# Who multiplies the modulation blocks by silu(c): VectorE before, GpSimd between its splits of the weights after

## The chip, the cores and the metric

One core of one Trainium2 chip runs the whole program in one launch. The metric is the device time of that core in microseconds (us), given as the median of the runs made. TensorE (PE) multiplies matrices into eight PSUM banks, VectorE (DVE), ScalarE (ACT) and GpSimd (POOL) work elementwise, and SyncE (SP) issues nearly all loads from HBM to SBUF. Each engine runs its own program in order, and they meet only through counting semaphores.

## The reference, cut to what matters

Four transformer-like layers follow each other over 512 tokens of width 1024. The first two are modulated by a conditioning vector `c` of 1024 numbers:

```python
def adaln(c, w_mod, b_mod):
    mod = jax.nn.silu(c) @ w_mod + b_mod      # (1, 1024) @ (1024, 6144)
    return jnp.split(mod, 6, axis=-1)

def layer_ab(x, c, ...):
    sh_m, sc_m, g_m, sh_f, sc_f, g_f = adaln(c, mod_w, mod_b)
    h = modulate(x, norm_mix, sh_m, sc_m)
    ...
    x = x + g_m[:, None, :] * (jnp.concatenate([y_a, y_b], axis=-1) @ w_out)
    h = modulate(x, norm_ffn, sh_f, sc_f)
    return x + g_f[:, None, :] * swiglu(h, wg, wu, wd)
```

So there are two products of a vector by a 1024x6144 matrix, one for each of the first two layers. All other matrix products are of 512 tokens by a weight matrix. Everything is float32.

## The kernel before, in words

**Panels.** All weights are cut into 378 panels of 128 output columns: a panel is 128 partitions by 8 blocks of 128 (512 KB). A matrix product in float32 is made of three products of rounded parts (`three`, L567 to L569): high by high, low by high, high by low. A panel is 8 x 3 = 24 matmuls of 128x512. For each panel p, SP loads `raw` (L475), ACT rounds it into `w_hi` (`split_hi`, L902), POOL subtracts to get `w_lo` (`split_lo`, L518), and PE multiplies (`panel`). `raw`, `w_hi` and `w_lo` have RING = 4 slots each. SP loads panel p + 4 once `lo_ready` says that panel p is split; ACT rounds panel p once PE has done panel p - 4.

**Modulation blocks.** The two modulation matrices are 96 blocks q of the same shape as a panel. The first 16 are loaded at the start into `first_mods` and are finished before the first panel: 10 of them go through VectorE, 6 through PE alone (`ALONE`). The other 80 are loaded into `modraw`, which has MRING = 2 slots, and are taken along beside the panels: `mods_beside(p)` gives two of them to each of the panels 0 to 5, and one to each of the panels 6 to 73. Block q is multiplied by silu(c) (`csil`, one number for each row of the matrix), in place, then summed over its 8 blocks k into `modsum` (4 slots), and one matmul with a column of ones (`mod_panel`, L582) sums over the partitions into column q of PSUM bank 7. Before the change, VectorE does both steps in `sum_mod`: the multiply is L1382, the sum L1387.

**Order on VectorE.** It works AHEAD = 2 panels in front: beside panel p it runs `sum_mods(p + 2)` and only then takes panel p out of its bank, by `copy_out` (L1175) in the input panels or `add_x` (L1230) in the projections. In the gate and up panels of the feed-forward part, both blocks of a pair come behind the pair's `prod` (L1271) and `g_lo` (L1286).

**Order on SP**, which the change does not touch, is written out:

```python
                    p = MOD_TWICE + j
                    load_raw(it * 4 + (p + RING), (p + RING) % RING, it * 4 + (p + 1))
                    load_mod(it * 4 + (q_first + j), (q_first + j) % MRING, it * 4 + summed(q_first + j - MRING))
```

The last argument of `load_raw` is what `lo_ready` must have reached, that of `load_mod` what `mod_summed` must have reached; `q_first` is the block beside panel 6. The loop for the panels 0 to 5 has the same order: first `load_raw(p + RING, after=p + 1)`, then the blocks of `mods_beside(p)`, each once block q - 2 is summed. Blocks 16 and 17 are loaded ahead of both.

**Stages.** Panels 0 to 17 are the input projection of layer 0 (16 and 17 together in `token_panels`), beside the causal convolution and the scan of the recurrent branch on VectorE (`lru_conv`, `lru_scan`); behind panel 15, VectorE lays out the blocks of the compression (`lay_blocks`) and PE multiplies them (`hidden`, L748). Attention follows, with no panel in it. Then come panels 18 to 25 (out projection, `project`), the norm (`rstd`, `norm_h`), and the feed-forward part: gate and up panels 26 to 41, down panels 42 to 49, gate and up 50 to 65, down 66 to 73, and the rest, 74 to 93, with no modulation block.

Of the kernel before, what the change touches and what calls it, by code (L numbers as in the profile page):

```python
# [15 lines left out]
ALU = mybir.AluOpType  # L16
# [3 lines left out]
P = 128  # L20
D = 1024
T = 512
KB = D // P
# [15 lines left out]
RING = 4  # L39
# [3 lines left out]
MRING = 2  # L43
# [9 lines left out]
P_OUT0 = P_VW + 1  # L53
# [8 lines left out]
P_AG = P_FFN1 + FFN_PANELS  # L62
# [50 lines left out]
def build(nc, A):  # L113
    with ExitStack() as ctx:
# [11 lines left out]
        def sem(name):  # L126
            return ctx.enter_context(nc.semaphore(name))
# [142 lines left out]
        panel_done = sem("panel_done")  # L270
        bank_free = sem("bank_free")
        mod_summed = sem("mod_summed")
        mod_used = sem("mod_used")
        csil_ready = sem("csil_ready")
        squares_ready = sem("squares_ready")
# [237 lines left out]
        @block.gpsimd  # L513
        def _(pool):
            def split_lo(p, slot):

                pool.wait_ge(hi_ready, p + 1)
                pool.tensor_tensor(w_lo[:, slot, :], raw[:, slot, :], w_hi[:, slot, :].bitcast(F32), ALU.subtract)\  # L518
                    .then_inc(lo_ready, 1)

            def split_from(p0, n):
                with pool.Fori(0, n // RING) as it:
                    for j in range(RING):
                        split_lo(it * RING + (p0 + j), (p0 + j) % RING)
                for p in range(p0 + n // RING * RING, p0 + n):
                    split_lo(p, p % RING)

            split_from(0, P_OUT0 + RING)

            pool.wait_ge(cmp_done, 2)  # L530
            pool.wait_ge(bank_free, P_OUT0)
            for br, src in enumerate((ksT, kwT)):
                for b in range(2):
                    pool.tensor_scalar(k0pad[:, br, b, :], src[:, :], own_half[:, b:b + 1], None, ALU.mult)
            pool.drain()
            pool.sem_inc(keys_padded, 1)
            split_from(P_OUT0 + RING, P_AG - P_OUT0 - RING)

            pool.wait_ge(layer2_landed, 48)
            pool.affine_select(out=wsT[:, :, :], in_=wsT[:, :, :], compare_op=ALU.is_ge, fill=0.0, base=0,  # L540
                               pattern=[[0, 8], [1, P]], channel_multiplier=-1).then_inc(ws_masked, 1)
            split_from(P_AG, P_U + RING - P_AG)

            for p in range(P_U + RING, P_OUT2 + RING):
                split_lo(p, p % RING)
                for k in taps_beside(p - RING):
                    pool.wait_ge(tap_made, k)
                    pool.tensor_tensor(cout[:, 3, :], cout[:, 3, :], tapped[:, k % 2, :], ALU.add).then_inc(tap_added, 1)
                    pool.drain()
            split_from(P_OUT2 + RING, P_OUT3 - P_OUT2)  # L550

            pool.wait_ge(bank_free, P_OUT3)
            for g_ in range(2 * KB):
                if g_ >= 2:

                    pool.wait_ge(score_ready, U_AT[2] + 4 * (g_ - 1))
                for b in range(2):
                    pool.tensor_scalar(k3pad[:, g_ % 2, b, :], k3[:, g_ % KB, :], own_half[:, b:b + 1], None, ALU.mult)
                pool.drain()
                pool.sem_inc(keys_padded, 1)  # L560
            split_from(P_OUT3 + RING, N_PANELS - P_OUT3 - RING)
# [605 lines left out]
        def _(dve):  # L1167
# [207 lines left out]
                                         in1=cols[:, own:own + KB], op0=ADD, op1=MUL)  # L1375
                dve.drain()

            def sum_mod(panel_, landed, landed_value, used, sum_slot):

                dve.wait_ge(landed, landed_value)  # L1380
                w = panel_.rearrange("p (k n) -> p k n", n=P)
                dve.tensor_tensor(w, w, csil[:, :].rearrange("p (k o) -> p k o", o=1).broadcast_to((P, KB, P)), MUL)  # L1382
                dve.drain()

                if used is not None:
                    dve.wait_ge(mod_used, used)
                dve.tensor_reduce(modsum[:, sum_slot, :], panel_.rearrange("p (k n) -> p n k", n=P), AX_X, ADD)\  # L1387
                    .then_inc(mod_summed, 1)

            def first_sums():  # L1390
                dve.wait_ge(csil_ready, 1)
                by_dve = [q for q in range(MOD_FIRST) if q not in ALONE]
                for n, q in enumerate(by_dve):
                    sum_mod(first_mods[q // 4][:, q % 4, :], first_landed[q // 4], 16,
                            by_dve[n - SUMS] + 1 if n >= SUMS else None, summed(q) % SUMS)

            def sum_mods(p):

                for q in mods_beside(p):
                    sum_mod(modraw[:, q % MRING, :], mod_landed[q % MRING], 16 * ((q - MOD_FIRST) // MRING + 1),  # L1400
                            q - SUMS + 1, summed(q) % SUMS)

            def sum_mod_loop(it, p):

                q = mods_beside(p)[0]
                sum_mod(modraw[:, q % MRING, :], mod_landed[q % MRING], it * 32 + 16 * ((q - MOD_FIRST) // MRING + 1),
                        it * 4 + (q - SUMS + 1), summed(q) % SUMS)


# [546 lines left out]
```

## Time and profile before

| | |
|---|---|
| median of 3 runs | 2950.18 us (2949.32 to 2954.04) |
| profiled execution | span of 2948.6 us from the first to the last instruction; no time of its own is listed beside the three runs |
| PE busy | 2599.6 us, 88% of the span |
| DVE busy | 1508.2 us, 51% |
| POOL busy | 1012.6 us, 34% |
| ACT busy | 920.0 us, 31% |
| POOL, the 378 splits (L518) | 929.5 us, 2465 ns each |
| DVE, 80 multiplies by silu(c) (L1382) | 132.7 us, 1658 ns each |
| DVE, 80 sums over k (L1387) | 159.1 us, 1989 ns each |
| modulation blocks end at | 772 us of the span |

Busy shares are means over the whole span; a stage is read from the windows and the timeline. Matmuls overlap, so the pace of a panel is the distance between the same row of two panels and not the sum of its matmuls. In a timeline a row ends with the idle time in front of it and what ended that, in brackets.

### The profile page before, as it was taken

What the parts mean: (1) busy time and instruction counts of PE and PEld (TensorE: products, weight loads), DVE (VectorE), ACT (ScalarE), POOL (GpSimd) and SP (SyncE); (2) the same over time, 40 slices, a digit from 0 to 9 for tenths busy, and PEclk for the clock granted to TensorE, in tenths of its full rate; (3) what the DMA queues carried; (4) which work ended last, traced back from release to release, by engine and by line L of the source; (5) the groups of instructions that cost most, each with busy time, mean ns of one, the idle gap of its engine ahead of it and who ended that gap; (6) DMA issues with size and microseconds to landing.
All of it is one profiled execution on the core that took longest, in us unless ns stands there. A gap on an engine that the chain in (4) does not pass through costs nothing.

```text
span 2948.6 us, 36164 instructions
## 1 busy us (share of the span) xinstructions
PE 2599.6 (88%) x12106; PEld 2114.6 (72%) x12106; DVE 1508.2 (51%) x2628; ACT 920.0 (31%) x1481; POOL 1012.6 (34%) x435
## 2 busy tenths in 40 slices
PE   4678898999989888999996817999998988899998
PEld 4568676787876776788885706788876867688886
DVE  6993567686423873211116983525245435452534
ACT  2140453322233263322233223423232245342222
POOL 1130003444442202344452612344443353343443
PEclk9895899999998999999997958999999999999999
DMA  6431003455331102232231202232332210122322
GB/s 252 164 135 65 1 16 133 173 178 184 123 107 50 65 1 86 72 99 94 93 107 57 72 14 64 79 95 90 100 101 71 79 44 1 64 91 95 100 88 76
DMA packets 71769, 263.76 MB, mean 89 GB/s; under 512 B 7920, under 2 KB 8560, under 8 KB 71024
## 3 DMA queue, kind: packets, MB, share of 16 engines
q1 hardware_dynamic: 68352, 251.01, 25.9%
q10 hardware_dynamic: 3312, 11.40, 1.1%
q8 instruction: 60, 0.98, 0.1%
q14 instruction: 45, 0.37, 0.0%
HBM read 260.28 MB, written 2.10 MB: 89 GB/s over the span
## 4 chain that ended last, share of the span: by engine, by line
PE 50%; issue 30%; DVE 8%; POOL 7%; DVEq 2%; ACT 2%; POOLq 1%; DMA 0%; SPq 0%; ACTq 0%
PE bank L567 15%; PE bank L568 14%; PE bank L569 14%; POOL w_lo L518 7%; DVE cout L1693 2%; PE bank L680 2%; PE bank L670 1%; PE bank L661 1%; DVE tn L1219 1%; DVE acc L1192 1%; ACT prob L983 1%; DVE h_lo L1214 1%; PE bank L824 1%; DVE modsum L1387 1%; DVEq L1686 1%
## 5 line engine op out<-in xcount | busy, mean ns | idle before, releaser
L518 POOL TENSOR_TENSOR w_lo<-raw,w_hi 128x1024 fp32r<-128x1024 f32 x378 | 929.5, 2465 | 1821.4 <-ACT w_hi L902 1820.6
L567 PE MATMUL bank<-h_hi,w_hi 128*128 128x512 f32 x2128 | 862.2, 405 | 53.2 <-DVE h_lo L1214 40.4
L568 PE MATMUL bank<-h_lo,w_hi 128*128 128x512 f32 x2128 | 840.5, 395 | 0.0
L569 PE MATMUL bank<-h_hi,w_lo 128*128 128x512 f32 x2128 | 839.3, 394 | 0.0
L902 ACT ACTIVATE w_hi<-raw 128x1024 fp32r<-128x1024 f32 x378 | 397.4, 1055 | 759.7 <-PE bank L569 719.5
L567 PEld LDWEIGHTS bank<-h_hi,w_hi 128*128 128x128 f32 x2128 | 406.1, 191 | 172.1 <-DVE h_lo L1214 48.1
L569 PEld LDWEIGHTS bank<-h_hi,w_lo 128*128 128x128 f32 x2128 | 406.5, 191 | 87.3
L568 PEld LDWEIGHTS bank<-h_lo,w_hi 128*128 128x128 f32 x2128 | 407.3, 191 | 84.3 <-issue 4.6
L567 PE MATMUL bank<-g_hi,w_hi 128*128 128x512 f32 x704 | 280.6, 399 | 5.8 <-DVE g_lo L1286 5.8
L568 PE MATMUL bank<-g_lo,w_hi 128*128 128x512 f32 x704 | 278.6, 396 | 0.0
L569 PE MATMUL bank<-g_hi,w_lo 128*128 128x512 f32 x704 | 278.5, 396 | 0.0
L947 ACT ACTIVATE g_hi<-prod 128x512 f32 x88 | 55.6, 632 | 460.3 <-DVE prod L1283 242.9
L1271 DVE TENSOR_TENSOR prod<-silu,bank 128x512 f32<-128x512 f32 x44 | 30.3, 688 | 292.4 <-PE bank L569 292.4
L1230 DVE SCALAR_TENSOR_TENSOR x<-bank,plain,x 128x512 f32<-128x512 f32 x64 | 48.0, 751 | 257.6 <-PE bank L569 257.6
L1387 DVE TENSOR_REDUCE modsum<-modraw 128x128 f32<-128x1024 f32 x80 | 159.1, 1989 | 8.6 <-issue 0.6
L567 PEld LDWEIGHTS bank<-g_hi,w_hi 128*128 128x128 f32 x704 | 132.4, 188 | 39.7 <-DVE g_lo L1286 8.4
L569 PEld LDWEIGHTS bank<-g_hi,w_lo 128*128 128x128 f32 x704 | 132.5, 188 | 32.3
L568 PEld LDWEIGHTS bank<-g_lo,w_hi 128*128 128x128 f32 x704 | 132.5, 188 | 31.3
L1382 DVE TENSOR_TENSOR modraw<-modraw,csil 128x1024 f32<-128x1024 f32 x80 | 132.7, 1658 | 6.6 <-DMA modraw<-in_mods 6.3
L1230 DVE SCALAR_TENSOR_TENSOR x<-bank,modv,x 128x512 f32<-128x512 f32 x64 | 47.7, 746 | 165.5 <-PE bank L569 165.5
L1693 DVE SCALAR_TENSOR_TENSOR cout<-pad,cols,cout 128x512 f32<-128x512 f32 x104 | 116.1, 1144 | 4.7 <-issue 0.4
L983 ACT ACTIVATE prob<-srow,stat 128x512 f32<-128x512 f32 (+1 forms) x192 | 106.5, 555 | 31.9 <-DVE stat L1348 31.7
(236 smaller groups left out, 2985.8 us busy)
## 6 DMA issues: line engine op xcount, KB each, us to landing
raw<-in_panels SPq DMA_DIRECT2D x378, 512.0 KB, 3.5
modraw<-in_mods SPq DMA_DIRECT2D x80, 512.0 KB, 3.5
first_mods<-in_mods SPq DMA_DIRECT2D x4, 2048.0 KB, 20.4
w<-in_w ACTq DMA_DIRECT2D x2, 2048.0 KB, 9.2
x<-in_x SPq DMA_DIRECT2D x1, 2048.0 KB, 8.5
out<-yout ACTq DMA_DIRECT2D x8, 256.0 KB, 2.2
mask<-in_causal ACTq DMA_DIRECT2D x1, 1024.0 KB, 4.8
mask<-in_dilated ACTq DMA_DIRECT2D x1, 1024.0 KB, 4.9
```

Source lines behind the costliest of these rows:

```text
L518: pool.tensor_tensor(w_lo[:, slot, :], raw[:, slot, :], w_hi[:, slot, :].bitcast(F32), ALU.subtract)\
L567: pe.matmul(out, w_h, m_h, start=start, stop=False)
L568: pe.matmul(out, w_h, m_l, start=False, stop=False)
L569: return pe.matmul(out, w_l, m_h, start=False, stop=stop)
L680: m = pe.matmul(bank[4 + n % 2][:, 0:HD], probT[:, n % 2, P * j:P * j + P], v_of(run, units[n], j), start=(j == 0), stop=(j == last))
L902: act.activation(w_hi[:, slot, :], raw[:, slot, :], ACT.Copy).then_inc(hi_ready, 1)
L947: act.activation(g_hi[:, it * 2 + a, :], prod[:, a, :], ACT.Copy).then_inc(f_hi_ready, 1)
L983: act.activation(prob[:, n % 3, 0:w], srow[:, n % 2, 0:w], ACT.Exp, bias=stat[:, 0, u % 64:u % 64 + 1], scale=SCALE, accum_out=stat[:, 1, ...
L1230: dve.scalar_tensor_tensor(out=x[:, n, :], in0=bank[p % RING][:, :], scalar=scale_by, in1=x[:, n, :], op0=MUL, op1=ADD).then_inc(bank_free, 1)
L1382: dve.tensor_tensor(w, w, csil[:, :].rearrange("p (k o) -> p k o", o=1).broadcast_to((P, KB, P)), MUL)
L1387: dve.tensor_reduce(modsum[:, sum_slot, :], panel_.rearrange("p (k n) -> p n k", n=P), AX_X, ADD)\
L1693: dve.scalar_tensor_tensor(out=cout[:, c, :], in0=pad[:, c, k:k + T], scalar=col("cconv", 4 * k + c), in1=cout[:, c, :], op0=MUL, op1=ADD)
```

## The change: GpSimd multiplies, VectorE sums

GpSimd's program gets a multiply of block q by `csil` behind the split of the panel that the block stands beside (`split_and_scale`, and `split_and_scale_from` as a loop of 4), with a wait on the block's load. A new semaphore `mod_scaled` counts these multiplies, and VectorE's sum waits for it in place of the load. The first 16 blocks stay as they were (`scale_first`). GpSimd also waits once, at the start, for `csil`.

```diff
--- before.py
+++ after.py
@@ -270,6 +270,7 @@
         panel_done = sem("panel_done")
         bank_free = sem("bank_free")
         mod_summed = sem("mod_summed")
+        mod_scaled = sem("mod_scaled")
         mod_used = sem("mod_used")
         csil_ready = sem("csil_ready")
         squares_ready = sem("squares_ready")
@@ -525,7 +526,34 @@
                 for p in range(p0 + n // RING * RING, p0 + n):
                     split_lo(p, p % RING)
 
-            split_from(0, P_OUT0 + RING)
+            def scale_mod(q, slot, landed):
+
+                pool.wait_ge(mod_landed[slot], landed)
+                w = modraw[:, slot, :].rearrange("p (k n) -> p k n", n=P)
+                pool.tensor_tensor(w, w, csil[:, :].rearrange("p (k o) -> p k o", o=1).broadcast_to((P, KB, P)), ALU.mult)\
+                    .then_inc(mod_scaled, 1)
+
+            def split_and_scale(p):
+
+                split_lo(p, p % RING)
+                for q in mods_beside(p):
+                    scale_mod(q, q % MRING, 16 * ((q - MOD_FIRST) // MRING + 1))
+
+            def split_and_scale_from(p0, n):
+
+                q0_ = mods_beside(p0)[0]
+                with pool.Fori(0, n // RING) as it:
+                    for j in range(RING):
+                        split_lo(it * RING + (p0 + j), (p0 + j) % RING)
+                        q = q0_ + j
+                        scale_mod(q, q % MRING, it * 32 + 16 * ((q - MOD_FIRST) // MRING + 1))
+                for p in range(p0 + n // RING * RING, p0 + n):
+                    split_and_scale(p)
+
+            pool.wait_ge(csil_ready, 1)
+            for p in range(MOD_TWICE):
+                split_and_scale(p)
+            split_and_scale_from(MOD_TWICE, P_OUT0 + RING - MOD_TWICE)
 
             pool.wait_ge(cmp_done, 2)
             pool.wait_ge(bank_free, P_OUT0)
@@ -534,7 +562,8 @@
                     pool.tensor_scalar(k0pad[:, br, b, :], src[:, :], own_half[:, b:b + 1], None, ALU.mult)
             pool.drain()
             pool.sem_inc(keys_padded, 1)
-            split_from(P_OUT0 + RING, P_AG - P_OUT0 - RING)
+            split_and_scale_from(P_OUT0 + RING, MOD_UNTIL - P_OUT0 - RING)
+            split_from(MOD_UNTIL, P_AG - MOD_UNTIL)
 
             pool.wait_ge(layer2_landed, 48)
             pool.affine_select(out=wsT[:, :, :], in_=wsT[:, :, :], compare_op=ALU.is_ge, fill=0.0, base=0,
@@ -1375,13 +1404,17 @@
                                          in1=cols[:, own:own + KB], op0=ADD, op1=MUL)
                 dve.drain()
 
-            def sum_mod(panel_, landed, landed_value, used, sum_slot):
-
-                dve.wait_ge(landed, landed_value)
+            def scale_first(panel_, landed):
+
+                dve.wait_ge(landed, 16)
                 w = panel_.rearrange("p (k n) -> p k n", n=P)
                 dve.tensor_tensor(w, w, csil[:, :].rearrange("p (k o) -> p k o", o=1).broadcast_to((P, KB, P)), MUL)
                 dve.drain()
 
+            def sum_mod(panel_, scaled, used, sum_slot):
+
+                if scaled is not None:
+                    dve.wait_ge(mod_scaled, scaled)
                 if used is not None:
                     dve.wait_ge(mod_used, used)
                 dve.tensor_reduce(modsum[:, sum_slot, :], panel_.rearrange("p (k n) -> p n k", n=P), AX_X, ADD)\
@@ -1391,19 +1424,20 @@
                 dve.wait_ge(csil_ready, 1)
                 by_dve = [q for q in range(MOD_FIRST) if q not in ALONE]
                 for n, q in enumerate(by_dve):
-                    sum_mod(first_mods[q // 4][:, q % 4, :], first_landed[q // 4], 16,
+                    scale_first(first_mods[q // 4][:, q % 4, :], first_landed[q // 4])
+                    sum_mod(first_mods[q // 4][:, q % 4, :], None,
                             by_dve[n - SUMS] + 1 if n >= SUMS else None, summed(q) % SUMS)
 
             def sum_mods(p):
 
                 for q in mods_beside(p):
-                    sum_mod(modraw[:, q % MRING, :], mod_landed[q % MRING], 16 * ((q - MOD_FIRST) // MRING + 1),
+                    sum_mod(modraw[:, q % MRING, :], q - MOD_FIRST + 1,
                             q - SUMS + 1, summed(q) % SUMS)
 
             def sum_mod_loop(it, p):
 
                 q = mods_beside(p)[0]
-                sum_mod(modraw[:, q % MRING, :], mod_landed[q % MRING], it * 32 + 16 * ((q - MOD_FIRST) // MRING + 1),
+                sum_mod(modraw[:, q % MRING, :], it * 4 + (q - MOD_FIRST + 1),
                         it * 4 + (q - SUMS + 1), summed(q) % SUMS)
```

GpSimd's program, in its loop of four splits for the panels 0 to 19, before:

```order
L518 TENSOR_TENSOR w_lo<-raw,w_hi 128x1024 [waits hi_ready]
L517 REGISTER_ALU
L518 TENSOR_TENSOR w_lo<-raw,w_hi 128x1024 [waits hi_ready]
L517 REGISTER_ALU
L518 TENSOR_TENSOR w_lo<-raw,w_hi 128x1024 [waits hi_ready]
L517 REGISTER_ALU
L518 TENSOR_TENSOR w_lo<-raw,w_hi 128x1024 [waits hi_ready]
```

and after, panels 0 and 1, which carry two modulation blocks each:

```order
L519 TENSOR_TENSOR w_lo<-raw,w_hi 128x1024 [waits hi_ready,csil_ready]
L533 TENSOR_TENSOR modraw<-modraw,csil 128x1024 [waits mod_landed0]
L533 TENSOR_TENSOR modraw<-modraw,csil 128x1024 [waits mod_landed1]
L519 TENSOR_TENSOR w_lo<-raw,w_hi 128x1024 [waits hi_ready]
L533 TENSOR_TENSOR modraw<-modraw,csil 128x1024 [waits mod_landed0]
L533 TENSOR_TENSOR modraw<-modraw,csil 128x1024 [waits mod_landed1]
```

In its loop for the panels from 6 on, with one block each, after:

```order
L519 TENSOR_TENSOR w_lo<-raw,w_hi 128x1024 [waits hi_ready]
L531 ISA
L533 TENSOR_TENSOR modraw<-modraw,csil 128x1024 [waits mod_landed0]
L518 REGISTER_ALU
L519 TENSOR_TENSOR w_lo<-raw,w_hi 128x1024 [waits hi_ready]
L533 TENSOR_TENSOR modraw<-modraw,csil 128x1024 [waits mod_landed1]
L518 REGISTER_ALU
L519 TENSOR_TENSOR w_lo<-raw,w_hi 128x1024 [waits hi_ready]
```

Between any two splits there is now one multiply, or two, each with a wait for a load into its slot of `modraw`.

VectorE's program, from the last `h_lo` of the first norm to the first panel taken out, before:

```order
L1214 SCALAR_TENSOR_TENSOR h_lo<-tn,modv,h_hi 128x512 [waits h_hi_ready] x2
L1382 TENSOR_TENSOR modraw<-modraw,csil 128x1024 [waits mod_landed0]
L1387 TENSOR_REDUCE modsum<-modraw 128x128 [waits mod_used]
L1382 TENSOR_TENSOR modraw<-modraw,csil 128x1024 [waits mod_landed1]
L1387 TENSOR_REDUCE modsum<-modraw 128x128 [waits mod_used]
L1382 TENSOR_TENSOR modraw<-modraw,csil 128x1024 [waits mod_landed0]
L1387 TENSOR_REDUCE modsum<-modraw 128x128 [waits mod_used]
L1382 TENSOR_TENSOR modraw<-modraw,csil 128x1024 [waits mod_landed1]
L1387 TENSOR_REDUCE modsum<-modraw 128x128 [waits mod_used]
L1382 TENSOR_TENSOR modraw<-modraw,csil 128x1024 [waits mod_landed0]
```

and after:

```order
L1243 SCALAR_TENSOR_TENSOR h_lo<-tn,modv,h_hi 128x512 [waits h_hi_ready] x2
L1420 TENSOR_REDUCE modsum<-modraw 128x128 [waits mod_used,mod_scaled] x6
L1204 COPY axp<-bank 128x512 [waits panel_done]
L1420 TENSOR_REDUCE modsum<-modraw 128x128 [waits mod_used,mod_scaled] x2
L1204 COPY axp<-bank 128x512 [waits panel_done]
L1420 TENSOR_REDUCE modsum<-modraw 128x128 [waits mod_used,mod_scaled] x2
L1204 COPY axp<-bank 128x512 [waits panel_done]
```

The multiplies are gone from between the sums, and each sum waits for `mod_scaled`, GpSimd's count. SP's program has the same rows before and after.

## Rows read from the trace of the kernel before

**Rows 1.** Five stretches: length, busy PE PEld DVE ACT POOL (instructions), PEclk, DMA share, GB/s.

```profile
core 0 of [0], span 2948.6 us
...
80.00:245.00 165.00, 118.04 (x493) 95.30 (x494) 152.78 (x121) 45.07 (x52) 39.32 (x16) 0.82 0.41 137
...
425.00:473.00 48.00, 46.49 (x206) 38.37 (x204) 38.01 (x29) 12.69 (x15) 17.47 (x8) 0.96 0.43 149
473.00:498.00 25.00, 14.55 (x47) 9.70 (x48) 16.38 (x26) 10.14 (x14) 1.95 (x1) 0.73 0.15 52
498.00:772.00 274.00, 272.64 (x1217) 220.20 (x1216) 201.54 (x139) 68.84 (x81) 126.03 (x47) 1.00 0.51 173
772.00:870.00 98.00, 98.00 (x431) 80.29 (x430) 18.09 (x26) 30.89 (x39) 47.81 (x20) 1.00 0.34 105
```

**Rows 2.** Windows of L1382 alone: length, DVE busy (instructions), PEclk, DMA share, GB/s.

```profile
...
80.00:245.00 165.00, 42.37 (x26) 0.82 0.41 137
...
```

**Rows 3.** Timeline, second down projection: start us, us, engine, line.

```profile
603.78 2.40 POOL L518 TENSOR_TENSOR w_lo<-raw,w_hi 128x1024 fp32r<-128x1024 f32 x1 [3.42 <-ACT w_hi L902]
604.08 3.18 DVE L1382 TENSOR_TENSOR modraw<-modraw,csil 128x1024 f32<-128x1024 f32 x1
607.33 2.00 DVE L1387 TENSOR_REDUCE modsum<-modraw 128x128 f32<-128x1024 f32 x1
608.26 0.28 PE L582 MATMUL bank<-ones,modsum 128*128 128x1 f32 x2
609.25 0.73 DVE L1230 SCALAR_TENSOR_TENSOR x<-bank,modv,x 128x512 f32<-128x512 f32 x1
614.08 0.28 PE L582 MATMUL bank<-ones,modsum 128*128 128x1 f32 x2
```

**Rows 4.** Timeline, out projection: the split of panel 22 and what it releases.

```profile
433.09 2.66 POOL L518 TENSOR_TENSOR w_lo<-raw,w_hi 128x1024 fp32r<-128x1024 f32 x1 [121.27 <-ACT w_hi L902]
435.92 0.33 SPq L475 DMA_DIRECT2D raw<-in_panels  x1
436.51 0.33 SPq L482 DMA_DIRECT2D modraw<-in_mods  x1
440.90 1.23 DVE L1382 TENSOR_TENSOR modraw<-modraw,csil 128x1024 f32<-128x1024 f32 x1 [2.53 <-DMA modraw<-in_mods]
```

**Rows 5.** Loads of modraw, 425 to 500 us.

```profile
...
DMA to landing us min/median/max: 4.1/4.3/4.8
```

**Rows 6.** Loads of modraw, 590 to 640 us.

```profile
...
DMA to landing us min/median/max: 3.4/3.4/3.9
```

**Rows 7.** Timeline of VectorE, start and end of the input panels.

```profile
81.13 1.22 DVE L1382 TENSOR_TENSOR modraw<-modraw,csil 128x1024 f32<-128x1024 f32 x1
221.84 1.87 DVE L1387 TENSOR_REDUCE modsum<-modraw 128x128 f32<-128x1024 f32 x1
223.62 0.68 DVE L1175 COPY kwT<-bank 128x512 f32<-128x512 f32 x1
```

**Rows 8.** Timeline of TensorE, the first products of the compression.

```profile
230.58 13.89 PE L748 MATMUL bank<-blocks,w 128*128 128x64 f32 x64 [26.47 <-issue]
```

**Rows 9.** Timeline of VectorE: last row of the out projection; g_lo of panels 26, 27.

```profile
472.90 0.74 DVE L1230 SCALAR_TENSOR_TENSOR x<-bank,modv,x 128x512 f32<-128x512 f32 x1
504.31 0.69 DVE L1286 TENSOR_TENSOR g_lo<-prod,g_hi 128x512 f32 x1 [0.93 <-ACT g_hi L947]
```

**Rows 10.** Timeline of GpSimd, the split of panel 30.

```profile
498.62 2.38 POOL L518 TENSOR_TENSOR w_lo<-raw,w_hi 128x1024 fp32r<-128x1024 f32 x1 [23.68 <-ACT w_hi L902]
```

**Rows 11.** Timeline of TensorE, the last modulation matmul, then panel 74.

```profile
772.10 0.28 PE L582 MATMUL bank<-ones,modsum 128*128 128x1 f32 x2
```

**Rows 12.** Timeline of TensorE, two matmuls in a row behind an idle stretch.

```profile
115.35 0.63 PE L568 MATMUL bank<-h_lo,w_hi 128*128 128x512 f32 x1
115.78 0.63 PE L569 MATMUL bank<-h_hi,w_lo 128*128 128x512 f32 x1
```

**Rows 13.** Instructions of L548: ns min/median/max.

```profile
L548 POOL TENSOR_TENSOR cout<-cout,tapped x16: 1507/1710/1841, 1650.6 to 1706.5; 128x512 f32<-128x512 f32 x16
```

## The prediction

> **What bounds the kernel now.** I first took the windows by stage. In the input panels (80 to 245 us) VectorE is busy for 152.8 of 165 us and TensorE for 118.0: VectorE sets the pace there [rows 1]. From 498 to 772 us TensorE is busy for 272.6 of 274 us at full clock, with VectorE at 201.5 and GpSimd at 126.0 [rows 1]: a wait of VectorE costs nothing there. The reader should see that the multiplies leave a tight VectorE in the first stretch only: 42.4 us in 26 instructions [rows 2].
>
> Then the pace of a panel. The modulation matmul that ends a panel stands at 608.26 and the next at 614.08 us: 5.82 us a panel [rows 3]. Within them GpSimd splits once, 2.40 us. Its period therefore has 3.4 us free, and a multiply as long as a split would fit by busy time: 4.8 us in 5.82. What decides is not the busy time but what each instruction waits for, so I followed one modulation block from the split to its first use.
>
> The split of panel 22 runs from 433.09 for 2.66 us, to 435.75. SyncE then issues the load of `raw` at 435.92 and that of `modraw` at 436.51, and VectorE's multiply, which waits for it, begins at 440.90 [rows 4]. So from the end of a split to the arrival of the block that stands beside the same panel there are **5.15 us**: 0.76 to issue, 4.4 to land. The loads of this stretch, issued in such pairs, landed in 4.1 to 4.8 us [rows 5]; loads issued apart from a `raw` load took 3.4 us [rows 6]. In the kernel before nobody feels this, since VectorE uses block q(p) two panels behind the split of p, and GpSimd does not wait for it.
>
> **What the change makes of it.** GpSimd now runs split(p), multiply q(p), split(p + 1), in this order. Multiply q(p) waits for a load that SyncE issues only once `lo_ready` has counted split(p). GpSimd therefore waits out each load, with the next split queued behind the wait. Its period is 2.40 (split) + 5.2 (issue and landing) + 2.4 (multiply) = **10.0 us a panel**, against 5.7 to 5.8 for TensorE. TensorE cannot begin panel p before split(p). The two slots of `modraw` don't help, as the order of SyncE's program and not a lack of slots holds the load back.
>
> The multiply on GpSimd is not in the trace. It has the size and the number of inputs of a split, so I take the split's 2.40 us [rows 3]. Its lower bound is the same 2.40, since no row shows GpSimd faster on that size. Its upper bound is 3.0 to 3.7: twice the 1.51 to 1.84 us of GpSimd's in-place 128x512 addition [rows 13], of which part is waiting for VectorE. The Trainium skill (GPSIMD Engine Reference, Performance versus the Vector engine) gives about 2.6 cycles an element for two inputs at 1.2 GHz, an estimate of 2.2 us for 1024; with it the sum would be 14 us lower over 72 multiplies. The split's own 2.40 us, above it, decides.
>
> For the wait I take 5.2 us. The bounds are 4.2 (0.76 + 3.4, if it lands like a load issued apart) and 5.6 (0.76 + 4.8).
>
> *Input panels.* GpSimd gets through split 0, both blocks, split 1, and then waits for block 18, whose load needs block 16 summed; that is behind the norm, as before. VectorE is free at 81.1 [rows 7]. It sums block 16 (2.0), the load lands 3.5 later at 86.6, two multiplies end at 91.4 (the second load lands meanwhile), and split(2) begins there. Panels 2 to 5 with two blocks take 2.4 + 5.2 + 4.8 = 12.4 each, 49.6 together, to 141.0; panels 6 to 17 take 10.0 each, 120, to 261.0; with the sum, 263.0. Before, the same sum ended at 223.7 (221.84 + 1.87), followed by the copy and the layout that let `hidden` begin at 230.58 [rows 7, 8]. That is **+39.3 us**. The multiplies taken off VectorE give nothing back, since it now waits for GpSimd: per panel its sum, copy and scan, some 7 us, lie inside the 10. The blocks of panels 18 to 21 are multiplied under `hidden`, the token panels and the attention, where GpSimd was idle; nothing is late there.
>
> *Out projection* (times as before, without the 39.3). Split(22) ends at 435.75 as before, as its `w_hi` waits for panel 18. Multiply 22 ends at 443.35 and each further one 10.0 later: that of panel 27 at 493.35, its sum at 495.35. `sum_mods(27)` stands ahead of `add_x(25)`, the last row of the projection, which began at 472.90 [rows 9]. Nothing of the norm can begin without it: **+22.4 us**. The splits themselves stay ahead of TensorE up to panel 25, so the projection loses nothing else. During the norm GpSimd catches up with panels 28 and 29; its rows may hold up an `h_lo` of the norm once, some 2 us, which I leave out of the sum.
>
> *Feed-forward.* Split(30) waits for panel 26: 498.62 before [rows 10], 521.0 now, to 523.4. Its block needs the sum of block q(28), which stands behind `g_lo` of panel 27 (504.31 + 0.69 before [rows 9], 527.4 now): sum to 529.4, load to about 533.0, multiply to 535.4, split(31) to 537.8. From there 10.0 each: split(74) ends at 537.8 + 430 = 967.8. TensorE's three panels of lead are used up at about panel 34. Panel 74, the first without a block, began behind the modulation matmul of 772.10 [rows 11], so 195.7 of which 22.4 is counted: **+173.3 us**. From 74 on split follows split in 2.4 us and TensorE is at its old pace. `prod`, `g_lo` and `add_x` run later behind their sums, by under 10 us, while a bank is needed again only four panels later; they hide there. Nothing after 93 touches the change.
>
> Sum: 39.3 + 22.4 + 173.3 = 235 us over the span of 2948.6. The median of the runs is 1.6 us above that span, so 2950.2 + 235 = **3185 us**, 8% slower.
>
> **The rivals.**
>
> *VectorE's relief shows (faster).* If a block were there when its split ends, GpSimd would need 4.8 us a panel and keep up, and the stretch from 80 to 245 us would lose up to the 42.4 us of multiplies [rows 2]: 2908 us. It turns at a wait of 0.9 us (5.7 less 4.8). Against it stand 5.15 us in [rows 4] and a SyncE program that has not moved. 2%; that the relief and the waits cancel within the measurement, 1%.
>
> *GpSimd's multiply is dearer*: in place and with a repeated operand it may go like the additions of [rows 13], at 3.1 us. With 22 multiplies in series in the input panels, 6 in the projection and 44 in the feed-forward, 72 x 0.7 = 50: 3235 us. 11%.
>
> *The block lands sooner*, at 4.2 us behind the split: 16 + 6 + 43 = 65 waits x 1.0: 3120 us. Fewer loads run at once than before, which speaks for it; the pair of loads issued together, as in [rows 5], against. 8%.
>
> *TensorE's clock becomes the limit.* It is starved for 4 us in each 10. Behind an idle stretch two matmuls start 0.43 us apart [rows 12], the level of 1.2 GHz, and the granted clock was 0.82 in the stretch where TensorE idled 28% of the time [rows 1]. If it stayed at the low level, a panel would take 24 x 0.43 + 0.3 = 10.6, over the 10.0, and the 40 panels from 34 on would add 0.6 each less the lead: 3205 us. The Trainium skill (TensorE: Matmul & The Clock Gate, The HAM clock gate) says that the throttled state is the default and activity releases it, which would allow this. 6%.
>
> The Trainium skill (GPSIMD Engine Reference, Key points) also says that GpSimd shares its SBUF interfaces with VectorE instructions that have two SBUF inputs. The multiply of VectorE that met a split took 3.18 us [rows 3] and the free one 1.22 [rows 7]. That speaks against the change, but with VectorE waiting anyway it moves no term.
>
> **How the numbers follow.** The forecast gets 72%: 3185 us. The range runs from 3125 to 3250: low end at the shorter wait, high end at the dearer multiply with a little of the longer wait (65 x 0.4 = 26). A measurement here can tell 0.2%, 6 us. Faster by more than that: 0.02; within: 0.01; slower: 0.97.
>
> **What would show it.** GpSimd's idle time ahead of its new multiply should be some 5 us, ended by the load of `modraw`, about 65 times; the gap between two splits 10.0 us from panel 34 to 73; VectorE idle ahead of its sums, ended by GpSimd; TensorE at about 55% from 560 to 1000 us, waiting for `w_lo`; `hidden` at about 270 us, panel 74 at about 1007. The forecast is wrong if the splits follow each other in under 6 us, or if SyncE's load of `modraw` is issued ahead of the split beside it.

## The result, and the profile after

| | before | after |
|---|---|---|
| median of the runs | 2951.86 us (4 runs, 2949.32 to 2954.04) | 3156.78 us (4 runs, 3147.57 to 3162.48) |
| profiled execution | span 2948.6 us | span 3145.8 us, time 3147.57 us |
| PE busy | 2599.6 us | 2662.9 us |
| DVE busy | 1508.2 us | 1364.0 us |
| POOL busy | 1012.6 us | 1144.6 us |
| mean granted clock | 0.930 | 0.912 |

The ratio is 1.0696, with an interval of 1.0676 to 1.0715: 7.0% slower. The forecast was 3185 us with a range of 3125 to 3250. The sign, the mechanism and the range held; the size is 28 us under the forecast.

The page of the kernel after, its groups of instructions (busy us and mean ns, then idle time ahead of them and what ended it):

```profile
L519 POOL TENSOR_TENSOR w_lo<-raw,w_hi 128x1024 fp32r<-128x1024 f32 x378 | 911.4, 2417 | 1499.6 <-ACT w_hi L931 1498.8
...
L1420 DVE TENSOR_REDUCE modsum<-modraw 128x128 f32<-128x1024 f32 x80 | 155.0, 1943 | 402.1 <-POOL modraw L533 401.6
L533 POOL TENSOR_TENSOR modraw<-modraw,csil 128x1024 f32<-128x1024 f32 x80 | 153.5, 1922 | 412.1 <-DMA modraw<-in_mods 412.1
```

VectorE lost its 132.7 us of multiplies and got 401.6 us of waiting for GpSimd. GpSimd got 153.5 us of multiplies and 412.1 us of waiting for the loads. The waits of the kernel after (total us, times, longest) show how regular that is, and how it goes on from engine to engine:

```profile
POOL modraw L533 <- DMA modraw<-in_mods: 412.1, 74, 23.1
DVE modsum L1420 <- POOL modraw L533: 401.6, 68, 8.1
...
PE bank L611 <- DVE modsum L1420: 134.6, 65, 4.1
```

One turn of the loop in GpSimd's timeline, second feed-forward part (start, length, and in brackets the idle time ahead):

```profile
598.90 2.36 POOL L519 TENSOR_TENSOR w_lo<-raw,w_hi 128x1024 fp32r<-128x1024 f32 x1
606.44 1.90 POOL L533 TENSOR_TENSOR modraw<-modraw,csil 128x1024 f32<-128x1024 f32 x1 [5.19 <-DMA modraw<-in_mods]
608.30 2.36 POOL L519 TENSOR_TENSOR w_lo<-raw,w_hi 128x1024 fp32r<-128x1024 f32 x1
615.72 1.90 POOL L533 TENSOR_TENSOR modraw<-modraw,csil 128x1024 f32<-128x1024 f32 x1 [5.06 <-DMA modraw<-in_mods]
```

And SyncE's queue between the first two of them:

```profile
601.43 0.33 SPq L476 DMA_DIRECT2D raw<-in_panels  x1
602.02 0.33 SPq L483 DMA_DIRECT2D modraw<-in_mods  x1
```

The split ends at 601.26, `raw` is issued 0.17 us later, `modraw` at 602.02, and the multiply begins at 606.44, 5.18 us behind the split. The next split stands behind it. This is the chain of [rows 4], now with GpSimd waiting inside it. From the split at 598.90 to that at 608.30 it takes 9.4 us. In the kernel before, a panel took 5.82 [rows 3].

The ends of the stages in the kernel after, from the timelines of TensorE, GpSimd, VectorE and TensorE again:

```profile
258.39 13.88 PE L777 MATMUL bank<-blocks,w 128*128 128x64 f32 x64 [24.75 <-issue]
```

```profile
452.17 2.40 POOL L519 TENSOR_TENSOR w_lo<-raw,w_hi 128x1024 fp32r<-128x1024 f32 x1 [122.02 <-ACT w_hi L931]
...
552.49 2.41 POOL L519 TENSOR_TENSOR w_lo<-raw,w_hi 128x1024 fp32r<-128x1024 f32 x1
...
953.52 2.35 POOL L519 TENSOR_TENSOR w_lo<-raw,w_hi 128x1024 fp32r<-128x1024 f32 x1
```

```profile
511.97 0.73 DVE L1259 SCALAR_TENSOR_TENSOR x<-bank,modv,x 128x512 f32<-128x512 f32 x1
```

```profile
965.41 0.49 PE L596 MATMUL bank<-h_hi,w_hi 128*128 128x512 f32 x1 [0.18 <-DVE x L1259]
```

- Input panels: `hidden` begins at 258.39 in place of 230.58 [rows 8], +27.8.
- From there to the split of panel 22: 452.17 in place of 433.09 [rows 4], so 8.7 us come back. The cause is below, in the section on what the runs showed.
- Out projection: its last row at 511.97 in place of 472.90 [rows 9], +39.1, of which 20.0 arose here.
- Feed-forward: panel 74 begins at 965.41. Before it began behind the modulation matmul of 772.10 [rows 11], at 772.24: +193.2, of which 154.1 arose here. The splits of panels 31 and 73 are 401.03 us apart, 42 periods of 9.55 us on average; single ones take 9.1 to 10.4.
- The rest: 197.2 - 193.2 = +4.0.

The windows of the kernel after, with the columns of [rows 1]:

```profile
80.00:245.00 165.00, 113.87 (x426) 86.55 (x426) 79.57 (x78) 45.06 (x51) 76.99 (x37) 0.84 0.35 119
560.00:960.00 400.00, 305.21 (x1096) 234.17 (x1095) 108.42 (x83) 60.59 (x71) 176.92 (x84) 0.86 0.32 110
```

No engine is full in either stretch. VectorE is busy for 79.6 us where it was busy for 152.8 [rows 1], the load share of 0.35 is lower too, and the time is longer. Between 560 and 960 us GpSimd has the highest share beside TensorE, and that is 44%. A loop of waits bounds the kernel, and only the timeline shows it.

### The profile page after: what moved, and what is told of

Its sections match the earlier page's. It is cut to its first block, busy times and chain, and to the rows that moved or that the text cites. A ratio compares the mean times of both kernels' runs of the same rounds, so it can differ in the third digit from the quotient of the medians.

```text
span 3145.8 us, 36170 instructions
## 1 busy us (share of the span) xinstructions
PE 2662.9 (85%) x12106; PEld 2149.4 (68%) x12106; DVE 1364.0 (43%) x2548; ACT 919.4 (29%) x1481; POOL 1144.6 (36%) x515
## 4 chain that ended last, share of the span: by engine, by line
PE 38%; issue 36%; POOL 14%; DVE 7%; DVEq 2%; ACT 2%; DMA 1%; POOLq 1%; ACTq 0%; SPq 0%
POOL w_lo L519 11%; PE bank L596 11%; PE bank L597 11%; PE bank L598 11%; POOL modraw L533 3%; DVE cout L1727 2%; PE bank L709 1%; PE bank L699 1%; PE bank L690 1%; DVE tn L1248 1%; DVE h_lo L1243 1%; ACT prob L1012 1%; PE bank L853 1%; DVE modsum L1420 1%; DMA modraw<-in_mods 1%
## 5 line engine op out<-in xcount | busy, mean ns | idle before, releaser
L519 POOL TENSOR_TENSOR w_lo<-raw,w_hi 128x1024 fp32r<-128x1024 f32 x378 | 911.4, 2417 | 1499.6 <-ACT w_hi L931 1498.8
L596 PE MATMUL bank<-h_hi,w_hi 128*128 128x512 f32 x2128 | 879.2, 413 | 54.7 <-DVE h_lo L1243 40.3
L597 PE MATMUL bank<-h_lo,w_hi 128*128 128x512 f32 x2128 | 855.5, 402 | 0.0
L598 PE MATMUL bank<-h_hi,w_lo 128*128 128x512 f32 x2128 | 853.1, 401 | 0.0
L596 PEld LDWEIGHTS bank<-h_hi,w_hi 128*128 128x128 f32 x2128 | 415.5, 195 | 177.8 <-DVE h_lo L1243 48.0
L598 PEld LDWEIGHTS bank<-h_hi,w_lo 128*128 128x128 f32 x2128 | 415.8, 195 | 91.2
L597 PEld LDWEIGHTS bank<-h_lo,w_hi 128*128 128x128 f32 x2128 | 416.7, 196 | 87.4 <-issue 4.7
L1420 DVE TENSOR_REDUCE modsum<-modraw 128x128 f32<-128x1024 f32 x80 | 155.0, 1943 | 402.1 <-POOL modraw L533 401.6
L533 POOL TENSOR_TENSOR modraw<-modraw,csil 128x1024 f32<-128x1024 f32 x80 | 153.5, 1922 | 412.1 <-DMA modraw<-in_mods 412.1
L611 PE MATMUL bank<-ones,modsum 128*128 128x1 f32 x180 | 35.5, 268 | 134.6 <-DVE modsum L1420 134.6
L611 PEld LDWEIGHTS bank<-ones,modsum 128*128 128x128 f32 x180 | 32.0, 214 | 159.7 <-issue 111.8
```

Of the source, the lines that this page charges most:

```text
L533: pool.tensor_tensor(w, w, csil[:, :].rearrange("p (k o) -> p k o", o=1).broadcast_to((P, KB, P)), ALU.mult)\
L596: pe.matmul(out, w_h, m_h, start=start, stop=False)
L597: pe.matmul(out, w_h, m_l, start=False, stop=False)
L598: return pe.matmul(out, w_l, m_h, start=False, stop=stop)
L611: pe.matmul(out, modsum[:, slot, :], ones[:, 0:1], start=True, stop=True).then_inc(mod_used, 1)
```

## The experiments

Each median below is set against runs of the kernel before that were made beside it on the same chip. The kernels of the first two experiments ran on one chip, those with the wait alone, the squared block and the two halves on a second, the rest on a third.

**The order of the two loads.** The first pair moves SyncE's load of the block ahead of that of `raw`, in both loops, in the kernel after and in the kernel before. A block's load then waits only for its slot, and no longer for the split beside it.

```diff
-                    load_raw(it * 4 + (p + RING), (p + RING) % RING, it * 4 + (p + 1))
                     load_mod(it * 4 + (q_first + j), ...
+                    load_raw(it * 4 + (p + RING), (p + RING) % RING, it * 4 + (p + 1))
```

In the kernel after:

> Only SyncE's order is changed against the kernel after: in each turn the load of the modulation block stands ahead of the load of raw, so it is no longer behind the wait for the split beside it. If the serial loop split, load, multiply is the cost, block q(p) is on its way while GpSimd multiplies the block before it and splits p: two panels take 2.4 + 5.2 + 1.9 = 9.5, 4.75 us a panel, under TensorE's 5.7, and all of the 205 us come back. The input panels may then show VectorE's relief, some 20 us: 2932 us, between 2915 and 2955. If the loss were GpSimd's own added work or the traffic on the SBUF ports, the time would stay over 3100 us.

In the kernel before:

> The same swap of the two loads in the kernel before, with VectorE still multiplying. VectorE uses a block two panels after its split, so an earlier load is worth little: 2952 us, within 6 of the kernel before. If the swap by itself were the gain of the run above, this one would be some 20 us faster too.

Measured: the changed kernel with the new order 2946.76 us (11 runs, 2937.03 to 2949.03), 0.9983 of before (0.9974 to 0.9992). The kernel before with the new order 2951.05 us (12 runs), 0.9998 (0.9989 to 1.0006). The order of two loads in SyncE's program takes back the whole 7%, and does nothing where GpSimd does not wait. The waits and a window of the changed kernel in the new order:

```profile
POOL modraw L533 <- DMA modraw<-in_mods: 120.7, 45, 23.2
```

```profile
80.00:245.00 165.00, 119.70 (x503) 97.81 (x504) 119.89 (x95) 46.74 (x53) 92.07 (x42) 0.82 0.44 146
520.00:780.00 260.00, 260.00 (x1174) 213.45 (x1173) 123.32 (x88) 64.95 (x76) 194.60 (x89) 1.00 0.53 178
```

In the feed-forward part TensorE is full at the full clock again, with GpSimd at 75%. This version beats both kernels, but the kernel before by only 0.17%. The relief of VectorE is in it (119.9 us busy for 152.8 of [rows 1]), but `hidden` begins at 228.60 for 230.58, where 33 us of VectorE's work are gone. Even these 2 us are no gain of the relief: in the kernel before with the new order, where VectorE still multiplies, `hidden` begins at 228.83. Where the relief went is the question of the last pair.

**One split between the load and its use.** GpSimd splits panel p + 1 before it multiplies the block beside p; SyncE stays as in the change.

```diff
+            split_lo(0, 0)
+            for p in range(P_OUT0 + RING):
+                if p + 1 < P_OUT0 + RING:
+                    split_lo(p + 1, (p + 1) % RING)
+                for q in mods_beside(p):
+                    scale_mod(q, q % MRING, 16 * ((q - MOD_FIRST) // MRING + 1))
```

(The same from panel 22 on.)

> SyncE's order as in the kernel after, but GpSimd multiplies the block beside panel p behind the split of panel p + 1, so that the load passes under a split. By the same sum two panels take 9.5 us: 4.75 a panel, TensorE sets the pace again, and the time is near that of the swap of the loads, 2920 to 2965 us. If not the wait but the multiply between two splits is what costs, it stays near 3157.

Measured: 2959.82 us (6 runs), 1.0031 of before (1.0019 to 1.0042). The loop is broken here too, at the other end, and 9.4 us remain. Where they come from, in the timelines of GpSimd, VectorE and TensorE:

```profile
258.70 2.34 POOL L519 TENSOR_TENSOR w_lo<-raw,w_hi 128x1024 fp32r<-128x1024 f32 x1 [38.53 <-ACT w_hi L938]
261.00 1.89 POOL L533 TENSOR_TENSOR modraw<-modraw,csil 128x1024 f32<-128x1024 f32 x1
```

```profile
262.93 1.91 DVE L1427 TENSOR_REDUCE modsum<-modraw 128x128 f32<-128x1024 f32 x1 [23.87 <-POOL modraw L533]
```

```profile
266.09 0.43 PE L801 MATMUL bank<-hid,w 128*64 128x32 f32 x4 [8.28 <-DVE vtok L1220]
```

The multiply of the block beside panel 19 now stands behind the split of panel 20, which waits until TensorE has done the token panels. VectorE holds its sum ahead of the copies that TensorE needs for the compression. That matmul ran at 258.81 in the trace of before: 7.3 us of the 9.4. The product behind it took 13.92 us for 12.01, most of the rest.

**The wait without the multiply.** GpSimd waits for the block and counts, and the product with silu(c) is left out.

```diff
-                pool.tensor_tensor(w, w, csil[:, :]..., ALU.mult)\
-                    .then_inc(mod_scaled, 1)
+                pool.sem_inc(mod_scaled, 1)
```

> The kernel after, where GpSimd waits for each of the 80 blocks and counts it, and multiplies none of them: the factor silu(c) is left out of these blocks. If the loop is serial, its period falls by the 1.90 us of the multiply, 72 times: 3157 - 137 = 3020 us, still 70 us slower than the kernel before, with nothing added but a wait. If the multiply's work were the whole cost, 2950 us.

Measured: 3040.95 us (4 runs) against 2949.88, 1.0300 (1.0283 to 1.0317). GpSimd's timeline:

```profile
603.67 2.36 POOL L519 TENSOR_TENSOR w_lo<-raw,w_hi 128x1024 fp32r<-128x1024 f32 x1 [5.70 <-DMA modraw<-in_mods]
611.44 2.41 POOL L519 TENSOR_TENSOR w_lo<-raw,w_hi 128x1024 fp32r<-128x1024 f32 x1 [5.42 <-DMA modraw<-in_mods]
```

The wait alone costs 91 us, with no new work on any engine. Its period is 7.8 us here, and 7.9 from panel 31 to 73, for 9.55 with the multiply: it falls by 1.6 to 1.7, where the multiply itself is 1.90, since the loads arrive a little later behind the split. Split 22 starts at 431.39 in this run, 1.7 us earlier than before [rows 4], and at 431.28 in a run below whose first 22 panels are as before: in the input panels, where VectorE was the bound, the wait by itself costs nothing, and all 91 us arise from panel 22 on. The other 116 us of the change (206.9, if its median is set against these runs of before) come with the multiplies that stand in the loop, on average 1.6 for each of the 72. The expected 3020 us, which gave each the full 1.90, was missed by 21 us.

**What a multiply costs there.** It took 1.90 us and the forecast had taken 2.40 from the split. Three kernels each changed one thing that differs between the two: the operand that is repeated (`csil`, replaced by `w`: the block is squared), the operation (subtract for multiply), and the type of the output.

```diff
-                pool.tensor_tensor(w, w, csil[:, :]..., ALU.mult)
+                pool.tensor_tensor(w, w, w, ALU.mult)
```

> The kernel after with the block multiplied by itself in place of the repeated csil, so silu(c) is left out and both operands are 1024 different elements. If the multiply took 1.90 and not 2.40 us because one operand stays the same for 128 elements, it now takes 2.40, and 72 of them in series add 36 us: 3193 us. If the type of the output or the operation made it cheaper, it stays at 1.90 and 3157 us.

```diff
-                pool.tensor_tensor(w, w, csil[:, :]..., ALU.mult)
+                pool.tensor_tensor(w, w, csil[:, :]..., ALU.subtract)
```

> The kernel after with subtract in place of multiply (the blocks become w - silu(c), so the factor is left out). The split is a subtraction and takes 2.36 to 2.40 us, the multiply 1.90. If the operation makes the difference, GpSimd's 80 instructions now take 2.4 us and the time rises by 72 x 0.5 to 3193. If the type of the split's output or its being out of place makes it, they stay at 1.90 us and the time at 3157.

```diff
-                pool.tensor_tensor(w, w, csil[:, :]..., ALU.mult)
+                pool.tensor_tensor(w.bitcast(F32R), w, csil[:, :]..., ALU.mult)
```

> The kernel after, with the multiply's output written as fp32r, the rounded type that the split writes, and nothing else changed. Two full operands and the subtraction both left the 1.90 us as they were; what is left of the difference to the split is its output: type, or written in another place. If the type makes it, the multiply takes 2.36 to 2.40 us, 72 of them in series add 35, and the time is 3190 us, nearer my forecast of 3185. If not, 1.90 us and 3155.

Measured: 3164.06, 3150.39 and 3155.36 us (4, 2 and 2 runs), 1.0714, 1.0676 and 1.0698 of before, with intervals of 0.2 to 0.3% to either side. The instruction itself (ns min/median/max), in the three kernels:

```profile
L533 POOL TENSOR_TENSOR modraw<-modraw x80: 1887/1893/2870, 56.4 to 979.5; 128x1024 f32<-128x1024 f32 x80
```

```profile
L533 POOL TENSOR_TENSOR modraw<-modraw,csil x80: 1889/1897/2877, 56.5 to 957.1; 128x1024 f32<-128x1024 f32 x80
```

```profile
L533 POOL TENSOR_TENSOR modraw<-modraw,csil x80: 1891/1899/2887, 56.3 to 972.1; 128x1024 fp32r<-128x1024 f32 x80
```

None of the three by itself is the reason: the median is 1.89 to 1.90 us each time. Two differences to the split (2417 ns mean in the kernel after) are left. The multiply writes over its own input, while the split reads two buffers and writes a third; and the code gives the multiply its block as 8 pieces of 128, the split its 1024 elements as one piece. Neither was tried by itself. That in place is quicker as such is doubtful: GpSimd's in-place addition takes 1.51 us at the least for half the elements [rows 13], though part of that may be waiting for VectorE. The reason stays open.

**Only half of the change.** In the first kernel GpSimd multiplies beside the panels 0 to 21 and VectorE from 22 on; in the second it is the other way round.

```diff
-            split_and_scale_from(P_OUT0 + RING, MOD_UNTIL - P_OUT0 - RING)
-            split_from(MOD_UNTIL, P_AG - MOD_UNTIL)
+            split_from(P_OUT0 + RING, P_AG - P_OUT0 - RING)
```

(VectorE's part, which in both kernels multiplies the blocks that GpSimd doesn't, is left out here.)

> GpSimd multiplies only the 28 blocks beside the panels 0 to 21; VectorE those beside 22 to 73, as in the kernel before. The loss of the input panels alone: the trace of the kernel after has hidden begin some 28 us later, so 2952 + 28 = 2980 us. If losses of the stages hid each other, it would differ from that.

```diff
-            for p in range(MOD_TWICE):
-                split_and_scale(p)
-            split_and_scale_from(MOD_TWICE, P_OUT0 + RING - MOD_TWICE)
+            split_from(0, P_OUT0 + RING)
```

> The converse: VectorE multiplies the 28 blocks beside the panels 0 to 21, GpSimd the 52 beside 22 to 73. 3157 - 28 = 3129 us, so that this loss and that of the run above add up to the whole 205.

Measured: 2982.6 us (4 runs), +32.7, 1.0114 (1.0097 to 1.0131); and 3130.55 us (4 runs), +180.7, 1.0615 (1.0598 to 1.0633). Together 213.4 us, for the 206.9 of the whole change. The two parts add, within the spread of some us between runs. `hidden` begins at 260.52 in the first and at 229.09 in the second, 31.4 us apart. In all, it begins at 258.4 to 261.0 in the five traces where GpSimd multiplies there with the old order of loads, and at 228.9 to 230.6 in the three where it doesn't. The +27.8 above, from two single traces, is thus the low end; the input panels lose 28 to 32 us.

**Where the relief of VectorE went.** The new order of loads comes again, once without the multiply (the product with silu(c) is left out, GpSimd waits and counts), and once whole, with GpSimd multiplying beside the panels 0 to 21 alone. Both edits are put together from those shown above: that of the loads, with that of the wait or that of the first half.

> The loads swapped as in e1_block_before_raw, and GpSimd only waits and counts, so the factor silu(c) is left out of the 80 blocks. It shows what VectorE's relief of 42 us is worth with nothing put on GpSimd. If GpSimd's multiplies give the relief back, because VectorE's instructions with two SBUF operands wait for them (the three taps of the first convolution took 7.37 us in e1 against 2.40), hidden begins at 215 to 220 us and the time is 2930 to 2937 us. If the relief is worth little because TensorE's pace and the chain of the scans set the end of the input panels, it stays at 2942 to 2947.

> The loads swapped, GpSimd multiplies beside the panels 0 to 21, VectorE from 22 on. From 22 on TensorE sets the pace whoever multiplies, so the gain of e1, if it is from the input panels, is kept: 2946 us, 2943 to 2950. If part of e1's gain were from the feed-forward stage, this is nearer 2950.

Measured: 2929.88 us (5 runs) against 2949.85, 0.9922 (0.9909 to 0.9936); and 2948.83 us (11 runs), 0.9986 (0.9976 to 0.9996). The first is 20.0 us under before, 19.0 under the second, which ran beside it, and 16.9 under the whole kernel in the new order, which ran on another chip. `hidden` begins at 210.48 there, 18.1 us before the 228.60. In this order of loads VectorE's relief is thus worth 20 us, and GpSimd's multiplies give back some 17 to 19 of them; at `hidden`, the end of the input panels, it is 18.1. Both points lie a little beyond what was expected (2930 us, `hidden` at 215).

The second was to show where the small gain of the new order comes from, and it came out nearer the 2950 that its expectation names as the sign of a gain in the feed-forward part than the 2946 forecast. Panel 74, in TensorE's timelines of the whole kernel in the new order and then of this one:

```profile
765.42 0.48 PE L596 MATMUL bank<-h_hi,w_hi 128*128 128x512 f32 x1
```

```profile
770.02 0.48 PE L595 MATMUL bank<-h_hi,w_hi 128*128 128x512 f32 x1
```

`hidden` begins at 228.60 and 228.46, and panel 74 is 4.6 us apart: in these traces, one of each, the gain arises behind the input panels, where GpSimd multiplies in the first and VectorE in the second. The kernel before in the new order has the same two points at 228.83 and 770.42. What the second has over before is no gain either. Four of its 11 runs lie at 2939 to 2942 us and seven at 2948 to 2952, a distance like that of the two clock levels of the last section.

VectorE's timeline at the first convolution, in the new order with GpSimd's multiplies and then without them:

```profile
131.49 0.55 DVE L1500 TENSOR_SCALAR xc<-axp,cols 128x512 f32<-128x512 f32 x1
132.11 7.37 DVE L1503 SCALAR_TENSOR_TENSOR xc<-axp,cols,xc 128x512 f32<-128x512 f32 x3
```

```profile
121.02 0.54 DVE L1499 TENSOR_SCALAR xc<-axp,cols 128x512 f32<-128x512 f32 x1
121.64 4.43 DVE L1502 SCALAR_TENSOR_TENSOR xc<-axp,cols,xc 128x512 f32<-128x512 f32 x3
```

GpSimd's timeline beside the first of the two:

```profile
131.86 1.93 POOL L533 TENSOR_TENSOR modraw<-modraw,csil 128x1024 f32<-128x1024 f32 x1 [0.68 <-DMA modraw<-in_mods]
133.75 2.78 POOL L519 TENSOR_TENSOR w_lo<-raw,w_hi 128x1024 fp32r<-128x1024 f32 x1
137.04 1.89 POOL L533 TENSOR_TENSOR modraw<-modraw,csil 128x1024 f32<-128x1024 f32 x1 [0.51 <-DMA modraw<-in_mods]
```

Of the 18.1 us, 10.5 are there at this point already. With two blocks a panel and two slots, a slot goes through load, multiply and sum, and each multiply of GpSimd is in that loop. That this loop makes the 10.5 us is read from the order and not tried with a third slot. The other 7.6 come behind it, of which these rows show 2.9: three operations with two inputs in SBUF took 7.37 us while GpSimd was at work nearly without a gap, 4.43 with one split beside them, and 2.40 in the trace of before at 134.42 with GpSimd idle. The operation with one input ahead of them is 0.55 and 0.54.

## Why the prediction was right, point by point

**What bounds after the change** was right: GpSimd's program, waiting for a load that SyncE issues behind the split beside it. The idle time ahead of the multiply, forecast at some 5 us about 65 times, is 412.1 us in 74; without the one of 23.1 at the start that is 5.3 each. The wait itself, forecast at 5.2 us from the end of the split, is 5.18 in the turn shown. That the order of SyncE's program and not a lack of slots holds the load back is shown by the first pair: with the same two slots, the reordered kernel is at 2946.76.

**The size of the multiply** is the term that was off. It was taken at 2.40 us "as the split", with that as its lower bound, and measured 1.90. The lower bound was no bound: one other instruction of the same size is a near row, not a limit. With 1.90 in the forecast's own sums, 22 multiplies take 11 us from the input panels (28.3; measured 27.8), 6 take 3 from the out projection (19.4; 20.0) and 44 take 22 from the feed-forward part (151.3; 154.1). Together these 36 us are more than the whole miss of 235 - 205 = 30. The sum would have been 199 us. The profiled execution has 197.2 and the medians 205; one stretch that met another level of the clock is of the size of that distance (last section). The Trainium skill (GPSIMD Engine Reference, Performance versus the Vector engine) gives about 2.6 cycles an element at 1.2 GHz, an estimate of 2.2 us for 1024. The trace has 1.90, and the measurement decides; the forecast had weighed that estimate and taken the value farther off.

**Input panels.** That the relief of VectorE gives nothing while it waits for GpSimd held. The experiments add what the forecast had not split. The wait alone costs nothing there (split 22 at 431.39). The multiplies without the serial wait cost nothing against before either (`hidden` at 228.46 to 228.60 in the new order). It takes both in one loop to pass what VectorE needed for a panel.

**Out projection and feed-forward.** Both steps held with the smaller multiply. The 42 periods take 9.1 to 10.4 us, where the forecast gave one length of 10.0; their mean of 9.55 is 0.45 shorter, nearly all of it the 0.50 of the multiply. That nothing behind panel 93 is touched held: from panel 74 to the end the two traces differ by 4.0 us. One sign was missed: TensorE was to be busy at about 55%, and from 560 to 960 us it is at 76% (305.21 of 400), because the forecast counted its panels at full clock.

**The rivals.** *Relief shows* fell for this kernel. Its price of 42.4 us was too high too: with the loads in the new order and no multiply on GpSimd it is 20 us. *Dearer multiply* fell, 1.90 and not 3.1. *The block lands sooner* fell: 5.18 in the turn shown, and the loads of `modraw` between 560 and 840 us landed 4.1 to 5.3 us behind their issue. *The clock becomes the limit* fell in the rows of one panel, TensorE's timeline of the kernel after:

```profile
610.79 0.49 PE L596 MATMUL bank<-h_hi,w_hi 128*128 128x512 f32 x1
...
613.08 0.63 PE L597 MATMUL bank<-h_lo,w_hi 128*128 128x512 f32 x1
613.51 0.63 PE L598 MATMUL bank<-h_hi,w_lo 128*128 128x512 f32 x1
...
617.52 0.39 PE L597 MATMUL bank<-h_lo,w_hi 128*128 128x512 f32 x1
617.74 0.39 PE L598 MATMUL bank<-h_hi,w_lo 128*128 128x512 f32 x1
```

Part of this panel runs at the level of 1.2 GHz (0.43 us from matmul to matmul) and the rest at 2.4 (0.23); the granted clock is 0.86 over the stretch. The panel takes 617.97 - 610.79 = 7.2 us for 5.7 before and still fits the 9.4. The clock is no cause of the loss: it is 1.00 in this stage as soon as the new order of loads keeps TensorE busy, and the period of GpSimd's loop has no term for it.

## What to carry to other kernels

Before a piece of work moves to an engine with room, follow what it waits for back to what issues that: if the issue waits for this same engine, the move closes a loop, and its period is the sum of all its parts whatever the busy shares say. Such a loop is opened by the order of two loads in the queue's program, or by one unit of other work between the load and its use, and that is to be looked at before the work is moved. Ask as well what the relieved engine and the new one share; here 17 to 19 of the 20 us that the relief was worth went back, in part that way and in part, it seems, through the two slots.

## What the runs showed of the hardware

- **GpSimd's multiply of a block is quicker than its split.** 1.89 to 1.90 us in the median for 128x1024, with multiply or subtract, one repeated operand or two full ones, and either type of output, against a mean of 2.42 for the split of as many elements. The reason is open.
- **VectorE beside GpSimd.** Three taps with two SBUF inputs: 2.40 us alone, 4.43 with one split beside them, 7.37 with splits and multiplies close together. The Trainium skill (GPSIMD Engine Reference, Key points) names this sharing without a price; the traces agree with it. What the taps lost beside the one split, 2.03 us, is a little less than the split's own 2.35. The sums, with one input, stay at 1.90 to 2.03 us from 86 to 127 us in both traces. So moving an elementwise operation from VectorE to GpSimd need not free all of its time on VectorE.
- **The clock at a stage that the change does not touch.** The 8.7 us that came back behind `hidden` are in these rows, TensorE's timeline of the kernel after:

```profile
287.73 7.36 PE L777 MATMUL bank<-blocks,w 128*128 128x64 f32 x64
...
294.93 3.74 PE L803 MATMUL bank<-kdiag,q 128*128 128x64 f32 x32
```

In the trace of before the same two took 12.01 and 7.03 us (granted clock 0.59 from 230 to 310 us; after, 0.67 from 258 to 338). In the profiled run of the squared block, which has the same program but for an operand, the first of them took 12.03 us again. From `hidden` to the split of panel 22 that run takes 202.4 us for 193.8 here, 8.6 of the 16.5 by which it is longer. The run with subtract has 7.36 and 3.74 us again, that with the rounded output 11.96 and 7.03. So kernels that differ in an operand meet one or the other, and the 8.7 us are no effect of the multiply's place that any run shows. It is also of the size by which the profiled execution, 3147.57 us, lies under the median of the runs after, 9.2 us; the other runs of the kernel after have no trace to show it. The 53 runs of the kernel before all lie at 2948.2 us or over, so it never showed this gain. What decides which level this stretch gets was not tried.
